# Second mixer of a two-layer encoder: low-rank outputs interleaved with value blocks, keys normalised bank by bank, gate weights split inside two tiles

## What is computed

```python
xr, xw, xk, xv, xa, xg = (h + xx * mu[i] for i in range(6))
r, k, v = xr @ w_r, xk @ w_k, xv @ w_v
g = sigmoid(xg @ g1) @ g2
lw = tanh(xw @ w1[z]) @ w2[z]            # z = 0, 1: forward, backward
decay = exp(-exp(-softplus(-(w0[z] + lw)) - 0.5))
a = sigmoid(a0[z] + (xa @ a1[z]) @ a2[z])
kk = k * k_k, divided by its norm in each head of 64
k_dir = k * (1 + (a - 1) * k_a);  b_dir = kk * a
S = S * decay + (S @ -kk) (x) b_dir + v (x) k_dir;  y = S @ r     # both directions
y = groupnorm(y) * ln_w + ln_b + bonus * v
out = (y * g) @ w_o
```

## Time and profile before

| what | us |
|---|---|
| runs | 1241.33, 1239.94, 1240.36; median 1240.36 |
| span of the profiled execution | 1240.2 |
| TensorE matmuls busy | 1198.4 (97%) |
| VectorE busy | 798.6 (64%) |
| ScalarE busy | 656.3 (53%) |
| GpSimd busy | 402.6 (32%) |
| x0 starts | 807.04 |
| x1 starts | 818.04 |
| tile 0's first product | 839.36 |
| tile 1's, tile 2's first product | 858.51, 879.82 |

### The profile page before, as it was taken

The page is one execution under the profiler, slowest core; times in us unless marked ns, Lnnn a source line. Parts: engine busy times, 40 slices in busy tenths (PEclk is TensorE's granted clock), DMA queues, the critical chain, the costliest instruction groups (busy, mean ns, idle before and its releaser), DMA issues.

```text
span 1240.2 us, 27516 instructions
## 1 busy us (share of the span) xinstructions
PE 1198.4 (97%) x11214; PEld 1088.6 (88%) x11214; DVE 798.6 (64%) x1272; ACT 656.3 (53%) x1114; POOL 402.6 (32%) x218
## 2 busy tenths in 40 slices
PE   7999999988999999999999989988999999999998
PEld 5899999876989999999999979977999888899998
DVE  7655555788685555585555479768777657755554
ACT  5545444654275445474554446684666544554452
POOL 0343443311123443424434410015343412334433
PEclk9999999999999999999999989998999999999999
DMA  9345445422255455554554544411000015554552
GB/s 362 135 171 203 170 185 203 153 103 102 103 209 198 165 190 199 187 209 175 196 195 163 200 152 154 154 52 54 4 4 4 3 65 193 205 203 164 191 195 93
DMA packets 18657, 188.00 MB, mean 152 GB/s; under 512 B 2064, under 2 KB 2576, under 8 KB 3600
## 3 DMA queue, kind: packets, MB, share of 16 engines
q1 hardware_dynamic: 18576, 186.84, 41.1%
HBM read 185.78 MB, written 1.05 MB: 151 GB/s over the span
## 4 chain that ended last, share of the span: by engine, by line
PE 82%; DVE 10%; ACT 5%; issue 1%; DMA 1%; SPq 0%; POOL 0%; DVEq 0%
PE gu_bank L265 23%; PE gu_bank L267 12%; PE bank L244 7%; PE bank L246 7%; PE bank L245 7%; PE bank L1459 7%; PE gu_bank L244 3%; PE gu_bank L1459 3%; PE gu_bank L246 3%; PE gu_bank L245 3%; DVE WL L199 2%; PE gu_bank L1490 2%; ACT WH L187 2%; DVE HX L405 1%; DMA raw<-stream_in 1%
## 5 line engine op out<-in xcount | busy, mean ns | idle before, releaser
L208 POOL TENSOR_TENSOR WL<-raw,WH 128x1024 fp32r<-128x1024 f32 x96 | 326.6, 3402 | 590.5 <-ACT WH L193 569.5
L265 PE MATMUL gu_bank<-HX,WH 128*128 128x512 f32 x1280 | 455.7, 398 | 1.8 <-DVE PL L546 1.8
L267 PE MATMUL gu_bank<-HX,WL 128*128 128x256 f32 x1280 | 359.5, 281 | 0.0
L199 DVE TENSOR_TENSOR WL<-raw,WH 128x2048 fp32r<-128x2048 f32 (+1 forms) x114 | 245.2, 2151 | 130.6 <-ACT WH L187 130.6
L265 PEld LDWEIGHTS gu_bank<-HX,WH 128*128 128x128 f32 x1280 | 240.7, 188 | 58.1 <-DVE PL L546 2.5
L267 PEld LDWEIGHTS gu_bank<-HX,WL 128*128 128x128 f32 x1280 | 241.9, 189 | 0.0
L187 ACT ACTIVATE WH<-raw 128x2048 fp32r<-128x2048 f32 (+1 forms) x114 | 205.1, 1799 | 26.4 <-PE gu_bank L246 14.4
L244 PE MATMUL bank<-PH,WH 128*128 128x256 f32 (+1 forms) x720 | 201.8, 284 | 1.0 <-ACT arena L2056 1.0
L245 PE MATMUL bank<-PL,WH 128*128 128x256 f32 (+1 forms) x720 | 201.7, 283 | 0.0
L246 PE MATMUL bank<-PH,WL 128*128 128x256 f32 (+1 forms) x720 | 201.6, 283 | 0.0
L244 PE MATMUL gu_bank<-HX,WH 128*128 128x256 f32 x464 | 137.2, 296 | 4.1 <-DVE HX L405 3.4
(11 more groups left out here) (313 smaller groups left out, 1823.1 us busy)
## 6 DMA issues: line engine op xcount, KB each, us to landing
raw<-stream_in SPq DMA_DIRECT2D x114, 1536.0 KB, 6.4
cst<-const_in SPq DMA_DIRECT2D x1, 1568.0 KB, 16.9
X<-xT_in SPq DMA_DIRECT2D x1, 1024.0 KB, 5.7
raw<-stream_in SPq DMA_DIRECT2D x1, 1024.0 KB, 7.7
arena<-hconst_in SPq DMA_DIRECT2D x2, 512.0 KB, 10.9
out<-X SPq DMA_DIRECT2D x4, 256.0 KB, 2.1
arena<-hconst_in SPq DMA_DIRECT2D x1, 768.0 KB, 13.7
arena<-fw_in SPq DMA_DIRECT2D x1, 512.0 KB, 8.5
```

The lines of the kernel that those rows point to most:

```text
L199: nc.vector.tensor_tensor(WL[:, slot, :cut], raw[:, slot, :cut], WH[:, slot, :cut].bitcast(fp32), ALU.subtract).then_inc(lo_ready, 1)
L208: (eng or nc.gpsimd).tensor_tensor(WL[:, slot, cut:end], raw[:, slot, cut:end], WH[:, slot, cut:end].bitcast(fp32), ALU.subtract).then_inc ...
L265: nc.tensor.matmul(out[:, :], WH[:, slot, w:w + P], HX[:, x, :, :].rearrange("p i t -> p (i t)"), start=k == 0, stop=False)
L267: return nc.tensor.matmul(out[:, L:2 * L], WL[:, slot, w:w + P], HH[:, x, :], start=False, stop=k == CT - 1)
```

## The change

- x0 and v3 are issued interleaved, and so are x1 and v5. The row block is a generator that gives one output tile (three matmuls) at a time. With lead = 4 for x0, v3's eight steps come after products 5, 6, 8, 9, 11, 12, 14 and 15; with lead = 8 for x1, one step of v5 comes after each of the products 8 to 15. v4 stays between x0 and x1.
- The spread of the norms moves from behind v5 into v6, ahead of v6's output tile 2.
- VectorE makes the removal keys of bank 2 (tiles 0 and 1) ahead of tile 0's betas, those of banks 3, 5 and 4 behind the queries. kk_ready counts banks; tile 0's direction products wait for 2, its further products for 3, its levels for 4.
- ScalarE makes all four value copies, in the order VB[3], VB[1], VB[2], VB[0]; VectorE makes none.
- The high parts of S_O are made in three pieces of 128 x 1024 by ScalarE: two at the end of levels 0 and 1 of tile 1, one at the end of level 0 of tile 2. The low parts: two pieces by VectorE at the end of levels 2 and 3 of tile 1, the third by GpSimd at the end of tile 2. Before, all were made ahead of tile 0.

The diff, cut to its core:

```diff
@@ pe_row_steps (the row block as a generator)
+                if m == CT - 1:
+                    last.then_inc(blocks_done, 1)
+                yield
@@ pe_lora_out
+        def pe_lora_out(pe, slot, b, k, values=(), lead=16):
+            steps = iter(values)
+            for n in range(16):
+                m, i, z = n // 4, n // 2 % 2, n % 2
+                q = 16 * k + n
...
+                last = three(x_bank(q), b * BLK + (4 * i + m) * P, slot, PH[r, i, :], PL[r, i, :], True, True, rows=r)
+                last.then_inc(lr_done, 1) if n < 15 else last.then_inc(blocks_done, 1)
+                for _ in range(CT * max(n + 1 - lead, 0) // (16 - lead) - CT * max(n - lead, 0) // (16 - lead) if lead < 16 else 0):
+                    next(steps)
@@ new
+        def pe_value_steps(pe, k):
+            g = MIX1_ORDER.index(f"v{k}")
+            s, b = S_RKV + g // 3, g % 3
+            wait_block(pe, s, b)
+            yield from pe_row_steps(pe, s % 2, b, VB, 2 * CT + k, k)
+        def pe_spread_norms(pe):
+            pe.wait_ge(kk_rec, 1)
+            pe.wait_ge(lr_ready, 32)
+            for j in range(CT):
+                nc.tensor.matmul(pair_half(XB, j), selt[:, j, :], RN[:, 1, :], start=True, stop=True).then_inc(kk_bc, 1)
@@ pe_mix1
+                if name == "v" and k in (3, 5):
+                    continue
...
+                    if k == 6:
+                        wait = lambda n: pe_spread_norms(pe) if n == 1 else None
...
-                    pe_lora_out(pe, slot, b, k)
+                    pe_lora_out(pe, slot, b, k, pe_value_steps(pe, 3 + 2 * k), (4, 8)[k])
...
-            pe.wait_ge(kk_ready, 1)
-            pe.wait_ge(vd_read, 1)
+            pe.wait_ge(kk_ready, 2)
             pe.wait_ge(va_read, 1)
@@ pe_tile
                 pe.wait_ge(va_read, 2)
+                pe.wait_ge(kk_ready, 3)
...
+            if isinstance(t, int) and t == 0:
+                pe.wait_ge(va_read, 4)
+                pe.wait_ge(kk_ready, 4)
@@ gate weights
+        GATE_HI, GATE_LO = [(1, 0), (1, 1), (2, 0)], [(1, 2), (1, 3)]
...
+                if (t, n) in GATE_HI:
+                    act_gate_high(act, GATE_HI.index((t, n)))
...
+                if (t, n) in GATE_LO:
+                    dve_gate_low(dve, GATE_LO.index((t, n)))
...
+            if t == 2:
+                split_last(pool, S_O, order=True)
@@ act_mix1, ahead of the tiles
-            next_hi(act, S_O)
             act.wait_ge(blocks_done, 3 * S_O)
-            A(V[:, 4 * L:6 * L], VB[2][:, :], cp).then_inc(va_read, 1)
-            A(V[:, 2 * L:4 * L], VB[1][:, :], cp).then_inc(va_read, 1)
-            act.wait_ge(vd_read, 2)
+            for j in (3, 1, 2, 0):
+                A(V[:, 2 * j * L:2 * (j + 1) * L], VB[j][:, :], cp).then_inc(va_read, 1)
+            act.wait_ge(va_read, 4)
@@ dve_mix1, ahead of the tiles
+            removal_keys(XB[0], (0, 1))
+            dve.wait_ge(kk_ready, 1)
...
             dve_query(dve, 0, 0)
-            next_lo(dve, S_O)
-            dve.wait_ge(blocks_done, 3 * S_O)
-            V_.tensor_copy(V[:, 6 * L:8 * L], VB[3][:, :]).then_inc(vd_read, 1)
-            V_.tensor_copy(V[:, 0:2 * L], VB[0][:, :]).then_inc(vd_read, 1)
+            for j in (1, 3, 2):
+                removal_keys(XB[j], (2 * j, 2 * j + 1))
+            dve.wait_ge(kk_ready, 4)
             dve_rb(dve, 0)
```

More of the change, by code:

```diff
@@ L1301, in build @@
         xt_ready, xt_hh, xt_hl = sem("xt_ready"), sem("xt_hh"), sem("xt_hl")
-        k_read, rp_read, va_read, vd_read = sem("k_read"), sem("rp_read"), sem("va_read"), sem("vd_read")
+        k_read, rp_read, va_read = sem("k_read"), sem("rp_read"), sem("va_read")
         omk_ready = sem("omk_ready")
@@ L1346, in pe_row_block, with pe_row_steps @@
         def pe_row_block(pe, slot, b, outs, i, k, wait=None):
+            for _ in pe_row_steps(pe, slot, b, outs, i, k, wait):
+                pass
+        def pe_row_steps(pe, slot, b, outs, i, k, wait=None):
             pe.wait_ge(mx_hl, i + 1)
@@ L1364, in pe_lora_in @@
             last.then_inc(blocks_done, 1)
[L1366 to L1383, removed]
+        def pe_lora_out(pe, slot, b, k, values=(), lead=16):
[3 more added lines that the diff above has]
+                q = 16 * k + n
+                if q == 0:
+                    pe.wait_ge(lr_lo, 2)
+                    pe.wait_ge(rp_read, 4)
+                elif q == 4:
+                    pe.wait_ge(hid_ready, 4)
+                elif q % 4 == 0:
+                    pe.wait_ge(lr_ready, q - 4)
+                r = slice(64 * z, 64 * z + 64)
+                last = three(x_bank(q), b * BLK + (4 * i + m) * P, slot, PH[r, i, :], PL[r, i, :], True, True, rows=r)
+                last.then_inc(lr_done, 1) if n < 15 else last.then_inc(blocks_done, 1)
+                for _ in range(CT * max(n + 1 - lead, 0) // (16 - lead) - CT * max(n - lead, 0) // (16 - lead) if lead < 16 else 0):
+                    next(steps)
         def pe_square_sums(pe):
@@ L1941, in dve_tile @@
                         dve_query(dve, t + 1, q)
+                    if isinstance(t, int) and t == 0:
+                        dve.wait_ge(va_read, 4)
                     dve_bonus(dve, t)
+                if (t, n) in GATE_LO:
+                    dve_gate_low(dve, GATE_LO.index((t, n)))
                 if ahead and n == 4:
@@ L2220, in dve_mix1, with removal_keys @@
             dve.wait_ge(k_read, 4)
[L2221 to L2225, removed]
+            def removal_keys(bank_, js):
+                dve.wait_ge(kk_bc, js[1] + 1)
+                for j in js:
+                    last = stt(out=KK[:, j * L:(j + 1) * L], in0=K[:, j * L:(j + 1) * L], scalar=pcol("k_k", j),
+                               in1=bank_[:, (j % 2) * L:(j % 2) * L + L], op0=ALU.mult, op1=ALU.mult)
+                last.then_inc(kk_ready, 1)
             V_.memset(small[:, 36:37], 0.0).then_inc(yt_ready, 1)
-            V_.memset(small[:, 37:38], 0.0).then_inc(kk_ready, 1)
+            removal_keys(XB[0], (0, 1))
+            dve.wait_ge(kk_ready, 1)
             dve.wait_ge(lr_ready, 32)
@@ L2379, in act_row_high, with act_gate_high @@
             nc.scalar.activation(WH[:, 1, c], raw[:, 1, c], ACT.Copy).then_inc((row_hi, hi_ready, hi_last)[b], 1)
+        def act_gate_high(act, b):
+            slot, c = S_O % 2, slice(b * BLK, (b + 1) * BLK)
+            if b == 0:
+                act.wait_ge(raw_full[slot], 16 * (S_O // 2 + 1))
+            ins = nc.scalar.activation(WH[:, slot, c], raw[:, slot, c], ACT.Copy)
+            if b:
+                ins.then_inc(hi_ready if b == 1 else hi_last, 1)
         def act_groupnorm(act):
@@ L2426, in dve_row_low, with dve_gate_low @@
                 .then_inc(row_lo, 1)
+        def dve_gate_low(dve, b):
+            slot, c = S_O % 2, slice(b * BLK, (b + 1) * BLK)
+            dve.wait_ge(hi_ready, S_O + 1)
+            ins = nc.vector.tensor_tensor(WL[:, slot, c], raw[:, slot, c], WH[:, slot, c].bitcast(fp32), ALU.subtract)
+            if b:
+                ins.then_inc(lo_ready, 1)
         def dve_groupnorm(dve, own):
@@ L2541, in _ @@
                 pool_operands(pool, 0, 0, part)
-            split_last(pool, S_O, order=True)
             pool.wait_ge(blocks_done, 3 * S_O)
```

2 lines of the change are left out of this document (removed).

## The result

| | before | after |
|---|---|---|
| median of the runs, us | 1240.84 (1239.94 to 1241.93, 4 runs) | 1263.37 (1263.16 to 1264.02, 4 runs) |
| ratio, 95% interval | | 1.0171 (1.0149 to 1.0192) |
| span of the profiled execution | 1240.2 | 1261.4 |
| mean granted clock | 0.990 | 0.981 |
| x0 starts | 807.04 | 807.75 |

The kernel became 22.5 us slower. The prediction said 7.2 slower, and its range ended at 1251. The reported time of an execution is 1.8 us longer than its span (1263.16 and 1261.4 for the one profiled here), so the two spans, whose difference is 21.2, are of two particular executions and not of the medians. The 21.2 us of the two spans fall apart so: 0.7 ahead of x0, 14.5 from x0's start to tile 0's first masks, -0.7 in tile 0, +5.5 in tile 1, +1.3 in tile 2, the rest (-0.1) after that.

What follows compares the result with a forecast made beforehand. TensorE was busy in 97% of the span, with ScalarE's sigmoids the pace in x0 and x1; 4.4 - 2.3 + 0.3 + 3.5 + 1.3 = +7.2 on 1240.2 + 0.1 gave about 1247.5 us, range 1237.5 to 1251.

Steps and rivals of the forecast that it cites:

- The groups of 0.55 us: In x0, three 128-row matmuls alone between two switches of row height take 0.55 us, not 0.36.
- The changes of mode: In x0 and x1, each TensorE switch between 64-row and 128-row matmuls costs 0.2 us; x1's last sigmoids come 8.6 later.
- tile 0 opens at full clock: TensorE stands 1.0 us instead of 3.54 ahead of tile 0, whose opening then takes 4.62 instead of 6.94: -2.3.
- The clock falls inside x1: Rival: TensorE's 2.5 us pause in x1 halves its clock, +8.9 to +10.6, giving 1249 to 1251 us; chance 0.12.
- The argument against: Against a clock fall in x1: its 2.5 us pause is shorter than 3.54, with half the work before and behind.
- The prediction's last sign of being wrong: Between x1 and tile 0: the forecast is wrong if the clock is at half anywhere between 821 and 848.
- Tile 1: 3.5 forecast: VectorE's two low pieces in tile 1 delay the gate product and the update behind it: 2.1 to 3.5 us, 3.5 taken.
- Tile 2: 1.3 forecast: GpSimd's low piece, 3.4 us at the end of tile 2, delays VectorE's second query or a bonus product: 1.3 taken.
- ScalarE's three pieces: Three pieces of 1.05 us at level ends in tiles 1 and 2 mostly hide: +0.3, ends nothing and 3.1.
- the weave works: Rival: interleaving v3 and v5 hides row-height switches in TensorE's existing pauses, 1235.5 to 1238 us; chance 0.15.
- 4.4: Tile 0 starts at 843.75 instead of 839.36 after the interleaving, keys by bank and moved spread: +4.4 us.
- Part 4: Gate weights in tiles 1 and 2: +0.3 for ScalarE, +3.5 for VectorE, +1.3 for GpSimd.

Runs made afterwards that it cites:

- the pause filled: Changed kernel with five v4 output tiles multiplied again between x1's products 23 and 24: ratio 1.0102 to the kernel before; with gate weights made before tile 0 too, 1.0032.
- the weave alone: Kernel before, with only v3 interleaved into x0 and v5 into x1: 1257.19 us, ratio 1.0119.
- the gate weights ahead: Changed kernel, interleaving kept, with all parts of S_O made ahead of tile 0 again: 1255.04 us, ratio 1.0095 to the kernel before.
- the coarse weave: Changed kernel with six value matmuls between products instead of three, S_O's parts made ahead of tile 0: 1243.58 us, ratio 1.0001 to the kernel before.
- x0 alone: Changed kernel with only v3 interleaved into x0, v5 as a block behind x1, S_O's parts made ahead of tile 0: 1246.55 us, ratio 1.0025.
- no weave: Changed kernel with v3 and v5 again as whole blocks behind x0 and x1, the rest kept: 1244.37 us, ratio 1.0012 to the kernel before.
- no weave, gate weights ahead: Changed kernel with v3 and v5 as whole blocks and S_O's parts made ahead of tile 0: 1239.52 us, ratio 0.9973; again on another chip 1239.6, 0.9974.
- the low part early: Kernel without interleaving, S_O made before tile 0, with GpSimd copying high parts and VectorE's low part ahead of its first removal keys: 1240.7 us, ratio 0.9982.

## Why the prediction was wrong

**The direction, and most terms, were right.** The groups of 0.55 us and the start of x1's sigmoids (822.15 forecast, 822.76 came, and x0 itself started 0.7 later) are in the trace. The changes of mode cost what the earlier trace rows says: with the pause filled, the last sigmoids are 8.6 us late, as worked out. That tile 0 opens at full clock holds too: from its first product to tile 1's first masks it takes 18.6 (855.53 to 874.14) instead of 20.3 (839.36 to 859.65), 1.7 less rather than the 2.3 priced from the earlier trace rows.

**The step that failed is the clock inside x1.** The sum puts it at nothing, and the rival "The clock falls inside x1" has a chance of 0.12 and a price of 1.7 to 3.4 us. The rival names the mechanism, with its place and its cause, but sizes it wrongly: 1.7 to 3.4 us of progress lost at half clock is a stretch of 3.4 to 6.8 us. The clock stayed at half for 27.3 us, until well into v7, and nearly everything in there is TensorE's pace. Counted from x0's start, the prediction has the last sigmoid at 26.0 and tile 0's first product at 36.7; after the change they came at 31.1 and 47.8. The 11.1 us are: the woven products to the last sigmoids 5.1 (31.12 less 26.04), the spread 3.5 (7.1, from 839.90 to v6's next matmul, less the 3.65 of the earlier trace rows), and the rest, 2.5, for 42 matmuls of v6 and v7, of which those before 852.7 start 0.21 apart instead of 0.12. The prediction's last sign of being wrong, the clock at half between 821 and 848, is what came. The term that was missing was how long the clock stays down, with its two other victims behind x1.

The chance was off as well. The argument against was that 2.5 us are shorter than 3.54, with half the work before and behind. The earlier trace rows show that 3.54 is enough, and nothing there said that 2.5 is not. The trace of the kernel before says more, read inside the pause, which ran from 835.83 to 839.36 (length, busy and count by engine, granted clock, DMA share, GB/s):

```profile
837.00:838.00 1.00, 0.00 (x0) 0.00 (x0) 1.00 (x1) 1.00 (x3) 0.84 (x1) 0.98 0.00 0
838.00:839.00 1.00, 0.00 (x0) 0.00 (x0) 1.00 (x2) 0.04 (x1) 1.00 (x1) 0.50 0.00 0
```

The clock was at half 2.2 us after TensorE had stopped, with 1.4 us of the pause still to come, so being shorter than 3.54 was no argument for the 2.5 us. Five kernels now show the fall behind pauses of 1.89 to 2.26 us in this place (the changed one, the weave alone, the gate weights ahead, the coarse weave, x0 alone), and three at pauses of 2.49 to 2.51 in tile 1 (the changed one, no weave, the pause filled), where the argument was not made at all.

**Tile 1: 3.5 forecast, 5.5 measured.** The wait was placed rightly, at the gate product behind VectorE's second piece. It made the product 2.9 late (894.64 is 20.50 behind the tile's first masks, 877.26 was 17.61), inside the bounds of 2.1 to 3.5. Missing was the clock again, for the other 2.6: 12 gate matmuls 0.21 apart instead of 0.12, the mean and the update at half speed. **Tile 2: 1.3 forecast, 1.3 measured**, in the way described: VectorE's second query took until GpSimd's low part ended. ScalarE's three pieces left no trace that could be told from nothing.

**The rival "the weave works"** needed changes of mode below some 0.07 us. They cost 0.2 wherever the trace shows one, and even half as many of them leave no gain (ratio 1.0001).

The sum, redone with what the runs showed: 4.4 - 2.3 + 0.3 + 3.5 + 1.3 from the prediction, +11.1 for the clock in x1, the spread and v6, +2.0 for tile 1, +0.6 for the smaller gain in tile 0, -0.3 for ScalarE's pieces, is +20.6. With the 0.7 that lies ahead of x0 it is 21.3, and the spans differ by 21.2. The last step, from span to time, was small and wrong too: 1240.2 + 0.1 takes the difference of one execution's span and the median of others, where an execution's own time is 1.8 above its span. And two ends don't come out of Part 4: the low ends of the pieces add up to 2.9 and not the 2.5 of the fast rival, and ScalarE's high end of 3.1 isn't in the upper bound. Neither touched the miss.

**What stays open.** Why the clock came back after 6.8 us in some kernels and after 24 to 27 in others wasn't settled. The long ones have v5 woven into x1 by threes behind an open pause; those by sixes, or with v5 on its own, have the short ones. Also open is why it falls at the spread in the kernels with the pause filled (836.6 and 836.8), with TensorE's 16-row matmuls under way and no pause above 0.5 us ahead of them. Without the weave it fell for 3.4 us during or behind the spread in three kernels (830.5, 831.0 and, with the low part early, 832.4); with the gate weights ahead of tile 0 it didn't fall in one execution and fell in tile 0 in the other. One trace per kernel is too little to say how often. That the long stretches belong to their kernels is better founded: the mean granted clock of every execution is 0.979 to 0.985 in the three kernels that have them, and 0.986 to 0.993 in the two with the pause filled.

## What to carry over

A pause of TensorE is not only its own length. Read the granted clock inside the pauses that the kernel already has, in steps of one us, before calling a shorter one safe. Work out what stands behind it that has TensorE as its pace, until the clock is seen to be back, and price all of that at half speed; an interleave that fills some pauses and leaves one of 2 us ahead of dense work can lose more than it wins. Interleaving products of different row heights costs 0.2 us at each change on this kernel, so count the changes and set them against the pauses that they fill. Take the parts of a combined change one by one: here one part was worth 0.3% and the other two hid it.

## What the runs showed of the hardware that was not expected

TensorE's clock stayed at 1.2 GHz for 27.3 us (twice) and 23.9 us while the trace shows it busy throughout or nearly (27.30, 26.49 and 23.90 busy). In other stretches of this region it was back after 3.4 to 6.9, once after 10.2. Being busy in the records is thus no sign that the clock will return. And the same kernel can have a fall in one execution and none in another (no weave, gate weights ahead).

Several VectorE operations with two inputs in SBUF that started behind a GpSimd operation took until about its end: the two queries of tile 2 took 2.96 where they take 0.80 in the earlier trace rows, GL took 2.40 instead of 0.69, and the two queries of tile 0 took 4.04 instead of 1.85. One of these GpSimd operations was a plain copy and not a subtraction: a cheap copy given to GpSimd is paid for on VectorE. GpSimd can pay too: in the kernel with no weave and the gate weights ahead its low part and VectorE's (2.28) started together at 833.2, and GpSimd's took 4.52, against 2.54 and 2.58 in the two traces where VectorE paid:

```profile
833.18 4.52 POOL L208 TENSOR_TENSOR WL<-raw,WH 128x1024 fp32r<-128x1024 f32 x1 [1.31 <-ACT WH L193]
```
